# Stick-breaking attention with five score banks, sums three units behind, and the next head's first operands made in the head before

## What is computed

```python
def stick_breaking(q, k, v, bias, q_pos, k_pos):
    z = jnp.einsum('bqhd,bkhd->bhqk', q, k) * (HEAD_DIM ** -0.5) + bias[None, :, None, None]
    mask = k_pos[None, :] < q_pos[:, None]
    log_keep = jnp.where(mask, jax.nn.log_sigmoid(-z), 0.0)
    later = lax.cumsum(log_keep, axis=3, reverse=True) - log_keep
    w = jnp.where(mask, jnp.exp(jax.nn.log_sigmoid(z) + later), 0.0)
    return jnp.einsum('bhqk,bkhd->bqhd', w, v)
```

## Time and profile before

| | us |
|---|---|
| median of 3 runs | 3800.48 |
| lowest and highest | 3800.01, 3808.25 |
| the profiled execution | 3792.23 |
| its span, first to last instruction | 3790.5 |
| attention: first scores of head 0 to the end of head 7 | 744.7 to 1835.0 |
| attention: values of the last sample row | 1835.0 to 1883.0 |
| one head inside the loop, first scores to first scores | 136.1 |

### The profile page before, as it was taken

How to read it: one execution, slowest core, us unless ns; L and a number is a source line. 1 busy time by engine, 2 the same in 40 slices (tenths; PEclk the granted TensorE clock), 3 DMA queues, 4 the chain that set the end, 5 groups by cost and what they waited for, 6 DMA issues and landing times. The chain is left out here.

```text
span 3790.5 us, 49656 instructions
## 1 busy us (share of the span) xinstructions
PE 3394.3 (90%) x14901; PEld 2324.8 (61%) x14901; DVE 2029.2 (54%) x2880; ACT 1407.5 (37%) x2206; POOL 493.0 (13%) x711
## 2 busy tenths in 40 slices
PE   4999865789898899889679979999999999999998
PEld 3888743333333333333268857778777877777777
DVE  5010138787788778779145545534553445345542
ACT  4110101256555555555233334423442344223332
POOL 1000010033333333333101100000000000000000
PEclk8999877699999999999779989999999999999999
DMA  4121251377797788788545543343334333443333
GB/s 122 62 72 44 78 76 26 95 226 227 254 311 248 255 287 264 255 266 298 187 147 148 155 113 91 94 146 105 94 99 141 106 95 100 139 121 119 123 113 113
DMA packets 487646, 569.68 MB, mean 150 GB/s; under 512 B 64807, under 2 KB 308615, under 8 KB 485320
## 3 DMA queue, kind: packets, MB, share of 16 engines
q1 hardware_dynamic: 482950, 549.81, 47.6%
q10 hardware_dynamic: 4328, 17.05, 1.2%
q0 software_dynamic: 176, 0.56, 0.0%
HBM read 506.91 MB, written 59.30 MB: 149 GB/s over the span
## 5 line engine op out<-in xcount | busy, mean ns | idle before, releaser
L2046 PE MATMUL ffn_bank<-ffn_xh,ffn_wh 128*128 128x512 f32 x1408 | 558.5, 397 | 19.3 <-DVE ffn_wl L2260 18.3
L2046 PE MATMUL ffn_bank<-ffn_xl,ffn_wh 128*128 128x512 f32 x1408 | 550.0, 391 | 0.0
L2046 PE MATMUL ffn_bank<-ffn_xh,ffn_wl 128*128 128x512 f32 x1408 | 549.3, 390 | 0.0
L1341 PE MATMUL att_bank<-att_X,att_negtri 128*128 128x512 f32 (+3 forms) x640 | 305.0, 559 | 65.2 <-POOL att_X L1085 52.8
L2046 PEld LDWEIGHTS ffn_bank<-ffn_xh,ffn_wh 128*128 128x128 f32 x1408 | 265.1, 188 | 95.9 <-DVE ffn_wl L2260 31.2
L1098 POOL TENSOR_TENSOR att_S<-att_S,att_X 128x512 f32<-128x512 f32 (+3 forms) x256 | 277.5, 1084 | 334.3 <-PE att_bank L1349 179.6
L1258 DVE TENSOR_REDUCE att_z_s<-att_prod 128x16 f32<-128x1024 f32 x256 | 313.0, 1223 | 8.7
L1253 DVE TENSOR_TENSOR att_prod<-att_Kr,att_bank 128x1024 f32<-128x1024 f32 x256 | 310.6, 1213 | 1.5 <-issue 1.5
L2046 PEld LDWEIGHTS ffn_bank<-ffn_xh,ffn_wl 128*128 128x128 f32 x1408 | 265.1, 188 | 56.1
L2046 PEld LDWEIGHTS ffn_bank<-ffn_xl,ffn_wh 128*128 128x128 f32 x1408 | 265.3, 188 | 52.1
L2264 DVE TENSOR_TENSOR ffn_wdl<-ffn_wdf,ffn_wdh 128x1024 fp32r<-128x1024 f32 x88 | 107.5, 1226 | 336.9 <-ACT ffn_wdh L2170 336.8
(11 more groups left out here) (362 smaller groups left out, 5704.7 us busy)
## 6 DMA issues: line engine op xcount, KB each, us to landing
att_Kr<-in_cache_k_dram SPq DMA_DIRECT2D x512, 256.0 KB, 3.7
att_Vr<-in_cache_v_dram SPq DMA_DIRECT2D x512, 256.0 KB, 3.8
ffn_wdf<-in_w_down_dram SPq DMA_DIRECT2D x108, 512.0 KB, 3.6
ffn_stage<-in_w_gate_dram SPq DMA_DIRECT2D x89, 512.0 KB, 3.9
ffn_stage<-in_w_up_dram SPq DMA_DIRECT2D x88, 512.0 KB, 4.5
qku_work<-in_x_prompt_dram SPq DMA_DIRECT2D x16, 512.0 KB
att_qf<-qT_dram SPq DMA_DIRECT2D x64, 128.0 KB, 3.4
att_kf<-kT_dram SPq DMA_DIRECT2D x64, 128.0 KB, 3.5
```

Source lines behind the costliest of these rows:

```text
L1341: last = pe.matmul(bank[:, u % 4, o:], negtri[:], X[:, u % NX, o:], start=False, stop=True, skip_group_check=True)
L2046: mm = pe.matmul(bank[:, first + f % 2, :], w[:, j, k, :], x[:, k, :], start=(k == 0 and n == 0), stop=(k == KD - 1 and n == 2))
```

## The change

- Scores go to five banks (`NZ` = 5), and z of unit s waits for Wt of unit s - 5. The two banks of the output follow behind (5 and 6); bank 7 stays with the sample row.
- PE's sums and ACT's weights run three units behind (`LAG` = 3), the product with V four, the output copies one step later than before.
- The splits of chunks 3 and 2 of the next head stand at steps 30 and 31 of the head that runs, the next bias at step 28. Chunk 1 of the head itself is split at step 1, chunk 0 at step 5. Head 0's first two chunks stand ahead of step 0.
- The query of the next sample row is spread by DVE at step 36, transposed by PE at step 37 into bank 7, and copied by ACT at step 38 to a new tensor `q_wide` in SBUF, from which L1253 now reads (L1292 in the new file). PE's values of the sample row run one step later.
- Head 7 is taken out of the loop, for it has no next head.
- SP's order is the same as before, and so is POOL's but for one memset.

```diff
-        NX, NW = 4, 4
+        NX, NW, NZ = 4, 4, 5
...
-        LAGS = 5
         K_END = NKK
+        LAG = 3
+        LAGS = LAG + 3
+        Q_AT = K_END + 5
...
-        SPLIT_AT = {0: 3, 1: 2, 5: 1, 9: 0}
+        SPLIT_NOW, SPLIT_NEXT = {1: 1, 5: 0}, {LAST[3] + 15: 3, LAST[2] + 4: 2}
+        BIAS_AT = LAST[3] + 13
...
-            with eng.Fori(1, H) as b:
-                body(b, range(NU), False, False)
-            body(H, range(LAGS), False, True)
+            with eng.Fori(1, H - 1) as b:
+                body(b, range(NU), False, False, False)
+            body(H - 1, range(NU), False, True, False)
+            body(H, range(LAGS), False, False, True)
...
+                def split(b, c):
+                    i = NCH - 1 - c
+                    cs = slice(c * CH, (c + 1) * CH)
+                    act.wait_ge(qk_loaded[i % 2], 64 * (b * (NCH // 2) + i // 2 + 1))
+                    if not (isinstance(b, int) and b == 0):
+                        act.wait_ge(z_ready, (b - 1) * NU + LAST[c] + 1)
+                    act.activation(qhh[:, cs], qf[:, i % 2, :], ACT.Copy).then_inc(qk_hi, 1)
...
+                def copy_queries(b):
+                    act.wait_ge(q_turned, b + 1)
+                    act.wait_ge(k_used, b * NKK)
+                    act.activation(q_wide[:], bank[:, S_B, :], ACT.Copy).then_inc(q_copied, 1)
...
-                        r, u = behind(b, s, 2, first, rest)
+                        r, u = behind(b, s, LAG, first, rest)
...
-                            tt(pr, Kr[:, kk % KSLOTS], bank[:, Q_B, :][:, None, :].to_broadcast([P, PP, AW]), ALU.mult
+                            tt(pr, Kr[:, kk % KSLOTS], q_wide[:, None, :].to_broadcast([P, PP, AW]), ALU.mult
...
-                            if not first or s >= 4:
-                                pe.wait_ge(w_ready, units_to(b, s, 4, first))
+                            if not first or s >= NZ:
+                                pe.wait_ge(w_ready, units_to(b, s, NZ, first))
...
-                        if s < NKK and not first:
-                            samples_v(b - 1, s)
+                        if 1 <= s <= NKK and not first:
+                            samples_v(b - 1, s - 1)
...
+                        if s == Q_AT and not last_head:
+                            turn_queries(b + 1)
```

More of the change, by code:

```diff
@@ new lines, in copy_queries, with round_ @@
+                def copy_queries(b):
+                    act.wait_ge(q_turned, b + 1)
+                    act.wait_ge(k_used, b * NKK)
+                    act.activation(q_wide[:], bank[:, S_B, :], ACT.Copy).then_inc(q_copied, 1)
+                for c in (3, 2):
+                    split(0, c)
+                copy_queries(0)
+                def round_(b, steps, first, last, rest):
+                    for s in steps:
+                        if not rest:
+                            for at in splits(b, s, first, last):
+                                split(*at)
@@ L1160, in round_ @@
                             act.activation(x_s[:], x_s[:], ACT.Ln, bias=1.0).then_inc(l_s, 1)
+                        if s == Q_AT + 1 and not last and not rest:
+                            copy_queries(b + 1)
                         if s == K_END + 5:
@@ L1201, in keep_sequence, with spread_queries, set_bias, split @@
                        ).then_inc(col_copied, 1)
[L1203 to L1206, removed]
-                    for s in steps:
[L1208 to L1214, removed]
+                def spread_queries(b):
+                    dve.wait_ge(q_turned, b)
+                    dve.tensor_copy(qrep[:], qsT[:, :, bass.ds(b, 1)].to_broadcast([P, QT, P])).then_inc(q_spread, 1)
+                def set_bias(b):
+                    dve.wait_ge(bias_ready, BP)
+                    dve.wait_ge(b_filled, b * NCH)
+                    dve.tensor_copy(bias_now[:], bias_rows[:, bass.ds(b, 1)]).then_inc(bias_now_ready, 1)
+                def split(b, c):
+                    i = NCH - 1 - c
+                    cs, low = slice(c * CH, (c + 1) * CH), slice(HD, P)
+                    dve.wait_ge(qk_hi, b * 3 * NCH + 3 * i + 3)
+                    tt(qlb[0:HD, cs], qf[0:HD, i % 2, :], qhh[0:HD, cs].bitcast(F32), ALU.subtract).then_inc(qk_lo, 1)
+                    tt(khl[low, cs], kf[low, i % 2, :], khl[low, cs].bitcast(F32), ALU.subtract).then_inc(qk_lo, 1)
+                set_bias(0)
+                spread_queries(0)
+                for c in (3, 2):
+                    split(0, c)
+                def round_(b, steps, first, last, rest):
+                    for s in steps:
+                        if not rest:
+                            for at in splits(b, s, first, last):
+                                split(*at)
                         def softplus():
@@ L1239, in round_ @@
                                 dve.wait_ge(alone_copied, r + 1)
[L1240 removed]
+                            tt(o_sb[:, c % 2, alone:], bank[0:HD, O_B + c % 2, alone:], o_odd[:, alone:], ALU.add).then_inc(o_copied, 1)
                         if rest:
@@ L1277, in round_ @@
                                                        ALU.mult, ALU.add).then_inc(r_s, 1)
+                        if s == Q_AT - 1 and not last:
+                            spread_queries(b + 1)
                         if s == K_END + 4:
```

88 lines of the change are left out of this document (42 added, 46 removed).

## The result

| | before | after |
|---|---|---|
| median, us | 3801.5 (3800.0 to 3808.3) | 3858.0 (3852.0 to 3867.0) |
| ratio, with its 95% interval | | 1.0154 (1.0130 to 1.0178) |
| the profiled execution | 3792.23 | 3859.46 |
| its span | 3790.5 | 3857.7 |
| head 7's first scores | 1698.55 | 1757.96 |

A forecast was written before the change was run, and what follows sets the result against it. The prediction took PE to set the pace. Looped heads +44, head 1 +6, head 7 +6 and head 0 +8 made +64 us, so 3864 us for the median, with a range of 3828 to 3905.

The forecast's parts named there:

- The load at step 1: Chunk 1's split at step 1 waits for a load landing at 17.1 us; PE idles 14.1 us where it idled 6.4.
- Unit 7: Chunk 0's load lands at 31.7 us, so PE idles 2.8 us before unit 7's scores, which start at 36.1.
- Step 33: DVE's splits and output copy delay the product PE awaits at step 33: 3.3 us idle, 1.5 of low clock.
- The old waits: PE's waits at head start (2.6 and 3.8 us), for softplus (8.2) and low clock (1.7) a head would go.
- The 120 us: PE's own work in a looped head, estimated as 136.1 less 2.6, 3.8, 8.2 and 1.7 us.
- Contention: DVE's product with two SBUF inputs and POOL hold each other up: 0 to 4 us a head, 0.5 taken.
- POOL loses as often as DVE: Reading of the skill's rule that whichever starts first keeps the other out; the sum was left unchanged by it.
- Five looped heads: Heads whose SP round enters through the loop's end: 144.9 us against 136.1, +8.8 each, +44 in all.
- Head 1: No loop jump in front of it, so 2.8 of the 3.5 us between L988 and L1018 come off: +6 us.
- head 0: Its chunk 1 load lands about when it did but is awaited at step 1, with K-steps 1 to 4 left: +8 us.
- head 7 and what follows: No loop jump, no next head's splits: +2.9 us at its start, +1 from the second load, one more unit to drain: +6.
- It works as meant: Rival: chunk 1's load is there when ACT reaches step 1, nothing stalls at steps 1 and 5: 3750 us, chance 0.07.

The follow-up runs named there:

- early loads: Changed kernel, but SP issues the loads of a head's chunks 1 and 0 behind the last page load of the head before: 3772.7 us, ratio 0.9927.
- a lag of two: Changed kernel with splits at 5, 9, 36 and 37, sums and weights two units behind, sample-row values at odd steps again, five banks kept: 3821.5 us, ratio 1.0065.
- late splits: Changed kernel with the splits of the head's own chunks 1 and 0 at steps 5 and 9, not 1 and 5: 3751.9 us, ratio 0.9859.
- the query in SBUF: Kernel before the change, plus ACT's copy of the spread query to SBUF, from which the product L1253 reads it: 3844.0 us, ratio 1.0118.

## Why the prediction was right, point by point

I forecast 3864 us and slower; the median was 3858.0, and in profiled executions +67.2 us where I had +64.

- **The load at step 1, right in mechanism and size.** Landing 17.1 us after the first scores: the last kf landed at 16.8 to 17.7 in looped heads. Scores of unit 3 at 20.9 with 14.1 us idle: 21.2 and 13.67. ACT idle for 12 to 16: 12.27. Heads 1 and 7, without the loop's end in front, landed at 14.9 and 13.9; L998 to the first L1028 took 0.6 us there and 3.3 to 3.4 in looped heads. The kernel with early loads took the whole stall away. The 2.7 us from L1028 to the first page, read in head 0, were 1329.64 - 1326.45 = 3.2.
- **Unit 7, right.** 2.8 us idle and the scores at 36.1: 2.01 and 36.7.
- **Step 33, within its bounds, wrong in part on the cause.** I had one wait of 3.3, for DVE's L1222, and 1.5 of low clock, 4.8 in all. There are two waits, 1.52 for a mask and 2.58 for L1222, and behind them the granted clock of head 4 is 0.73 over 2.7 us and 0.83 over the next 5.9, which costs about 1.7 (estimate): 5.8 in all. Moving the splits behind it took 2.8 back, moving the finish the rest of its wait.
- **The old waits, right, but for their size.** Those of the earlier trace rows are gone and step 21 fell from 5.25 to 2.55 us. I gave the waits in front of the softplus sums under 3 us a head, and heads 1 to 6 have 1.6. But the 8.2 us a head that I took off were 65.2 / 8, and head 0 alone has 21.2 of the 65.2: a looped head had about 6.1. So 2 us too many were taken from PE's own work. The 120 us came out right all the same (head 4 of the changed kernel: 146.7 less 20.5 of waits and, by an estimate from the granted clock behind them, 6.3 of low clock), so something else was too small by as much. No run shows what.
- **Contention, the step that failed.** "The price is then 0 to 4 us a head ... I take 0.5." I asked what it does to DVE's sequence, where 0.4 us a step are to spare, and took the mask of 0.83 us in the earlier trace rows as the size of POOL's loss. The mask's place was not in the sum: both it and the product follow softplus, the product 0.16 us ahead, so the product wins; the mask then takes 1.37 us; and PE waits for it, and pays again in clock. In the old schedule that is 6.4 us a head, outside my bounds. In the changed kernel the third unit of lag covers most of it (step 21 takes 2.55 us, and 7.79 with a lag of two), so little of the error reached the total, which was luck: nothing in my working said that the lag would cover it. At step 33 it does not. This is the mask that ends the wait of 1.52 us there in head 4, beside a product:

```profile
1441.60 1.22 DVE L1292 TENSOR_TENSOR att_prod<-att_Kr,att_q_wide 128x1024 f32<-128x1024 f32 x1
1441.76 1.37 POOL L1096 TENSOR_TENSOR att_X<-att_X,att_keepm 128x128 f32<-128x128 f32 x1 [2.00 <-DVE att_X L1263]
```

At 0.46 us it would have ended 0.9 earlier. What contention costs the changed kernel beyond that was not separated: no bank is free to put the query back.
- **The Trainium skill** (SBUF — State Buffer, Who interferes with whom, Practical consequences) has the rule that the one of the two that starts first keeps the other out. The traces agree, where the product starts first (mask 1.37 us for 0.45) and where POOL starts first (product 1.74 for 1.22). My sentence that "POOL loses as often as DVE" doesn't follow from the rule: the order in which the two are released decides, and here that is not by chance.
- **The parts.** Five looped heads: +44.1 (forecast 44), and that exactness is luck. I set 144.9 against 136.1, the time of one head; the five took 137.1 on average before and 145.9 after, so that both numbers were 1.0 too low. Head 1 +5.8 (6), head 0 +9.9 (8), head 7 and what follows +7.8 (6). The two terms that were small each, +1.9 and +1.8, are what is missing from the sum.
- **The rivals.** "It works as meant" was put at 3750 if the load were there in time. The kernel with early loads does that and took 3772.7; with the splits at 5, 9, 36 and 37 and PE's finish a step later, 3711 to 3720. So this rival's time was within reach of the schedule, by a few step numbers and SP's order, not of the change as made.

## What to carry to other kernels

A step that is moved earlier takes its inputs' arrival with it: when work moves forward by four steps, follow the queue that feeds it, issue by issue, to its landing, before counting any gain. A fixed order on two engines released by the same event is no random overlap: if they contend, the same one loses every time, and its loss counts in full where a third engine waits for it. A lag of one more step can hide such a loss. Of a wait that sits in an engine's own program order, as ACT's in front of the split, it hides only as much as the engine behind has work for: 2 to 3 us with late splits, but not 12. And a sum over the whole program, divided by the number of rounds, is not the price of a round: look first how much of it stands in the round that is unlike the others.

## What the runs showed of the hardware that I had not expected

- A product of two SBUF inputs stretched a 128x128 mask on POOL from 0.45 to 1.37 us, while the product kept its 1.22; with POOL first, the product took 1.74. A 128x512 sum of POOL and such a product held each other up too, and with 0.4 us a step to spare this cost PE nothing. A reduction with one input beside the mask left it at 0.47.
- At step 21 of the kernel before, PE waited 1.60 us in each of heads 1 to 7. Its matmuls ran on at a granted clock of 1.00 behind six of these waits, and at 0.62 over 4.54 us behind the seventh. With the query in SBUF the wait was 2.51 to 2.52, and behind all seven the clock was low: 0.67 over 4.3 us in six heads, 0.50 over 5.56 in one. That made 2.3 us of a delay of 0.9 in most heads.
- A wait of that length need not be followed by a low clock either: with a lag of two, step 5 of head 5 had a wait of 2.92 us and 1.00 over the 2.91 behind it, where head 3 had 2.93 and 0.50 over 5.55. So the price of one short wait can only be given as an average over heads.
